# Differential attention on one core: a values product per two query blocks, head norms gathered after the loop, Fourier terms ahead of the head terms

## The chip, the cores and the metric

The kernel runs on one core of a Trainium2 chip. The metric is the device time of one execution in microseconds (us). The engines are TensorE (PE in the rows; its weight loads are PEld), VectorE (DVE), ScalarE (ACT), GpSimd (POOL) and SyncE (SP), which issues most transfers.

## The reference, cut to what matters

Two blocks run one after the other on 512 tokens of width 1024: a convolution block with an MLP, then a block of two layers. The first of these layers holds differential attention with a Fourier mixer, and only that part is touched:

```python
def diff_attend(q, k, v, lam):
    s = jnp.einsum('bqhmd,bkhmd->bhmqk', q, k).astype(jnp.float32)
    p = jax.nn.softmax(s, axis=-1)
    a = p[:, :, 0] - lam * p[:, :, 1]
    return jnp.einsum('bhqk,bkhe->bqhe', a.astype(v.dtype), v)
...
def merge_even(att, f, subln, lam_init, w_out):
    b, n = att.shape[0], att.shape[1]
    att = rmsnorm(att, subln) * (1.0 - lam_init)
    o = jnp.concatenate([att.reshape(b, n, ATTN_V_W), fourier_mix(f)], axis=-1)
    return o @ w_out
```

There are 6 heads, 512 queries, 768 keys (512 tokens and 256 of context), two score maps per head with 64 channels each, and values of 128 channels. After the heads' norm over 128 channels, 768 attention channels and 256 Fourier channels go through an output projection of 1024 x 1024. Everything is fp32. A mixture of 16 experts follows, whose weights are most of what the kernel reads.

## The kernel before

Each engine has a program of its own, written out by hand, and they meet through counting semaphores. An engine does its instructions in order, so a waiting one holds up all behind it. A plain fp32 product shows as two passes in the rows (x12 for six products), a transpose as one.

The loop over `it` = 0 to 23 takes one query block of 128 rows of one head at a time (four blocks per head). For each block:

- TensorE makes the two score maps (`scores`, L1153) into three PSUM banks, two blocks ahead; the sets of two blocks alternate in banks 0 to 5.
- DVE takes the row maxima (`softmax_max`, L1561), one block ahead.
- ACT takes the exponentials with their sums (`exps`, L772), one block ahead.
- DVE combines the two maps (`combine`, L1573 to L1583) into `attn`.
- TensorE transposes the 768 key columns in six pieces (`attn_turn`, L1167), four into bank 6 and two into the first half of bank 7.
- ACT copies them to `aT` (`turn_in`, L781 and L783).

Per head, TensorE then makes the values product of 512 queries (`values`, L1174) into bank 7, queued ahead of the transposes of the next head's first block. ACT copies it to `o_sb` and squares it (`head_out`, L790 and L791), a product with a matrix of 1/128 gives the mean over channels on all 128 partitions (`head_stat`, L1182, bank 6), ACT takes the root (`head_root`, L795, which needs another function table than the exponentials), and DVE inverts it and scales the head into `hT` (`head_norm`, L1589 and L1590). These steps of a head stand in the queues of the next head's first two blocks, as here on TensorE:

```python
                if it and it % 4 == 0:
                    values(it // 4 - 1)
                if it > 4 and it % 4 == 1:
                    head_stat(it // 4 - 1)
                attn_turn(it)
```

After the last head the output projection makes eight tiles of 8 products each (`dense`, L903), of which products 0 to 5 take the heads and 6 and 7 the Fourier channels, ready since before the loop. DVE adds each tile to `xT` (L1407), ACT squares it for the next norm, POOL sums the squares, and L933 and L936 finish that sum. SyncE loads the first expert weights into the slots of a ring (`load_experts`) after the release of all projection tiles (L408).

Of the kernel before, what the change touches and what calls it, by code (L numbers as in the profile page):

```python
# [8 lines left out]
ALU = mybir.AluOpType  # L9
# [3 lines left out]
P = 128  # L13
D = 1024
DT = D // P
# [86 lines left out]
def block_kernel(nc, A, out):  # L102
# [137 lines left out]
    with ExitStack() as ctx:  # L240
# [85 lines left out]
        o_sb = carve(arena, 7680, N)  # L326
# [24 lines left out]
        for name in (  # L351
# [7 lines left out]
            "scores", "score_half", "neg_max", "probs", "attn_ready", "attn_turned", "aT_sb", "pv_done", "o_in", "o_stat", "o_rms",  # L359
            "o_ready",  # L360
# [33 lines left out]
        def _(sp):  # L394
# [8 lines left out]
            def load_experts(layer):  # L403
# [5 lines left out]
                if layer == 0:  # L409

                    sp.wait_ge(S["pv_done"], HEADS)
# [130 lines left out]
        def _(act):  # L542
# [233 lines left out]
            def turn_in(it):  # L776
                act.wait_ge(S["attn_turned"], it + 1)
                m = it % 4
                if m == 0 and it:
                    act.wait_ge(S["pv_done"], it // 4)  # L780
                act.activation(aT[:, 0:4, m * P:(m + 1) * P], psum[:, 6, :].rearrange("p (a b) -> p a b", a=4),  # L781
                               ACT.Copy).then_inc(S["aT_sb"], 1)
                act.activation(aT[:, 4:6, m * P:(m + 1) * P], psum[:, 7, 0:256].rearrange("p (a b) -> p a b", a=2),  # L783
                               ACT.Copy).then_inc(S["aT_sb"], 1)

            def head_out(h):
                act.wait_ge(S["pv_done"], h + 1)
                if h:
                    act.wait_ge(S["o_ready"], h)
                act.activation(o_sb, psum[:, 7, :], ACT.Copy).then_inc(S["o_in"], 1)  # L790
                act.activation(sq[:, 0, :], psum[:, 7, :], ACT.Square).then_inc(S["o_in"], 1)  # L791

            def head_root(h):
                act.wait_ge(S["o_stat"], h + 1)
                act.activation(rms[:, :], psum[:, 6, :], ACT.Sqrt, bias=eps[:, 0:1]).then_inc(S["o_rms"], 1)  # L795
# [12 lines left out]

# [80 lines left out]
        def _(pe):  # L889
# [268 lines left out]
            def attn_turn(it):  # L1158
# [622 lines left out]
```

## Time and profile before

| | |
|---|---|
| Median of 3 runs | 2569.98 us (2568.38 to 2574.26) |
| The profiled execution | 2574.75 us, its span 2573.0 us |
| Granted TensorE clock, mean | 0.965 |
| Busy in the span | TensorE 92%, DVE 27%, ACT 15%, POOL 2% |
| Head loop, from the first scores to the last combination | 154.60 us |
| From there to the first pass of the projection | 16.94 us |

Busy is the time in which an engine shows an instruction. The granted clock is a share of full speed: 1.00 is 2.4 GHz and 0.50 is 1.2 GHz. A wait is put down to the event that came last before the waiting instruction began.

### The profile page before, as it was taken

How to read it: one execution, taken by the hardware profiler on the slowest of the kernel's cores; microseconds unless marked ns; L12 is line 12 of the kernel's file. 1: busy time of each engine (PE TensorE's matmuls, PEld its weight loads, DVE VectorE, ACT ScalarE, POOL GpSimd, SP SyncE). 2: the span in 40 equal slices, each digit the busy share in tenths (PEclk: the TensorE clock that was granted, in tenths of full speed). 3: DMA queues.
4: the chain of work that ended last, by engine and by line, in shares of the span. 5: the costliest groups of instructions: out<-in, count | busy, mean ns of one | idle time of the engine just before them, and what ended most of it. 6: DMA issues, size and time to landing. Idle time of an engine off the chain costs nothing.

```text
span 2573.0 us, 21612 instructions
## 1 busy us (share of the span) xinstructions
PE 2366.4 (92%) x8882; PEld 1064.3 (41%) x8882; DVE 706.7 (27%) x958; ACT 376.4 (15%) x653; POOL 61.0 (2%) x66
## 2 busy tenths in 40 slices
PE   4999899999998999776969999999899879999997
PEld 2443344444444455443434444443344344444443
DVE  2683200000004760575141111112311231111113
ACT  1314200000003211354020000000200110000000
POOL 1000100000000000000100000000000100000000
PEclk8999999999999999987989999999999989999999
DMA  8307458218600010100069999998410269999995
GB/s 291 126 34 262 147 210 302 76 65 298 225 0 0 33 66 33 66 1 0 16 256 428 417 428 428 428 429 346 152 66 0 108 255 429 428 427 428 428 428 232
DMA packets 110554, 565.58 MB, mean 220 GB/s; under 512 B 8344, under 2 KB 8734, under 8 KB 85918
## 3 DMA queue, kind: packets, MB, share of 16 engines
q1 hardware_dynamic: 105856, 563.09, 54.1%
q10 hardware_dynamic: 4638, 1.64, 0.3%
q8 instruction: 44, 0.72, 0.1%
q14 instruction: 16, 0.13, 0.0%
HBM read 562.61 MB, written 2.10 MB: 219 GB/s over the span
## 4 chain that ended last, share of the span: by engine, by line
PE 80%; DMA 9%; DVE 6%; issue 2%; ACT 2%; SPq 1%; ACTq 0%; DVEq 0%
PE psum L903 39%; PE psum L1260 18%; DMA ring<-in_moe_w_gate_dram 7%; PE psum L1319 5%; PE psum L1275 5%; PE psum L1105 2%; PE psum L947 2%; DMA ring<-in_moe_w_down_dram 1%; PE psum L991 1%; PE psum L1174 1%; PE psum L923 1%; PE psum L1153 1%; DVE rstd L1395 1%; DVE rstd L1589 1%; PE psum L1218 1%
## 5 line engine op out<-in xcount | busy, mean ns | idle before, releaser
L903 PE MATMUL psum<-hT,ring 128*128 128x512 f32 x1632 | 717.7, 600 | 23.7 <-ACT hT L610 18.4
L1260 PE MATMUL psum<-ring,arena 128*64 128x512 f32 x3072 | 671.7, 595 | 21.6 <-DMA ring<-in_moe_w_gate_dram 14.3
L903 PEld LDWEIGHTS psum<-hT,ring 128*128 128x128 f32 x1632 | 312.4, 193 | 419.5 <-issue 412.6
L1260 PEld LDWEIGHTS psum<-ring,arena 128*64 128x64 f32 x3072 | 228.5, 137 | 450.4 <-issue 448.3
L903 PE MATMUL psum<-arena,ring 128*128 128x512 f32 x640 | 275.2, 592 | 0.0
L903 PEld LDWEIGHTS psum<-arena,ring 128*128 128x128 f32 x640 | 121.6, 190 | 153.1 <-issue 153.1
L1692 DVE TENSOR_TENSOR hT<-hT,psum 128x512 f32<-128x512 f32 x128 | 88.0, 687 | 245.6 <-PE psum L1319 245.6
L1275 PE MATMUL psum<-arena 128*128 128x128 f32 x1024 | 124.4, 282 | 2.5 <-DVE arena L1699 2.5
L1275 PEld LDWEIGHTS psum<-arena 128*128 128x128 f32 x1024 | 120.3, 197 | 14.0 <-issue 14.0
L1319 PE MATMUL psum<-arena 128*128 128x512 f32 x256 | 123.2, 619 | 0.0
L1407 DVE SCALAR_TENSOR_TENSOR xT<-psum,modv,xT 128x512 f32<-128x512 f32 x32 | 24.0, 751 | 308.5 <-PE psum L903 308.5
L1673 DVE TENSOR_TENSOR arena<-psum,arena 128x512 f32<-128x512 f32 x32 | 34.1, 1064 | 215.2 <-PE psum L1260 215.2
L1500 DVE TENSOR_TENSOR arena<-arena 128x512 f32<-128x512 f32 x32 | 22.2, 692 | 244.1 <-ACT arena L705 244.1
L947 PE MATMUL psum<-ring,cpad 128*32 128x512 f32 x576 | 66.0, 611 | 16.4 <-DMA ring<-in_w_mod_dram 16.4
L1167 PE MATMUL psum<-K,arena 128*128 128x128 f32 x144 | 29.6, 354 | 48.4 <-DVE arena L1583 33.3
L1319 PEld LDWEIGHTS psum<-arena 128*128 128x128 f32 x256 | 39.4, 188 | 83.5 <-DVE hT L1692 62.9
L597 ACT ACTIVATE sq<-xT 128x512 f32<-128x512 f32 x56 | 35.2, 631 | 260.3 <-DVE xT L1407 228.8
L1474 DVE SCALAR_TENSOR_TENSOR arena<-arena,vecT 128x512 f32<-128x512 f32 x90 | 72.3, 803 | 3.2
L1687 DVE COPY arena<-psum 128x512 f32<-128x512 f32 x16 | 11.1, 692 | 214.8 <-PE psum L1260 214.8
L705 ACT ACTIVATE arena<-psum 128x512 f32<-128x512 f32 x32 | 19.1, 598 | 311.7 <-PE psum L903 311.7
L829 ACT ACTIVATE arena<-psum 128x512 f32<-128x512 f32 x16 | 9.6, 599 | 365.7 <-PE psum L1275 365.7
L1518 DVE RECIPROCAL rstd<-rms 128x512 f32<-128x512 f32 (+1 forms) x18 | 50.8, 2820 | 44.0 <-ACT rms L744 43.9
(181 smaller groups left out, 1438.3 us busy)
## 6 DMA issues: line engine op xcount, KB each, us to landing
ring<-in_moe_w_gate_dram SPq DMA_DIRECT2D x64, 2048.0 KB, 14.9
ring<-in_moe_w_up_dram SPq DMA_DIRECT2D x64, 2048.0 KB, 16.7
ring<-in_moe_w_down_dram SPq DMA_DIRECT2D x64, 2048.0 KB, 16.8
ring<-in_ada_w_dram SPq DMA_DIRECT2D x24, 2048.0 KB, 10.5
ring<-in_mlp_w_dram SPq DMA_DIRECT2D x16, 2048.0 KB, 13.0
ring<-in_w_mod_dram SPq DMA_DIRECT2D x12, 2048.0 KB, 13.2
ring<-in_conv_w_pw_dram SPq DMA_DIRECT2D x6, 2048.0 KB, 18.5
ring<-in_conv_w_in_dram SPq DMA_DIRECT2D x6, 2048.0 KB, 18.8
```

Of the source, the lines that this page charges most:

```text
L597: act.activation(sq[:, g % 2, 0:width], src[:, j, :], ACT.Square).then_inc(S["sq_ready"], 1)
L903: ins = pe.matmul(bank[:, 0:width], w[:, k, col:col + P], src(k), start=start and k == 0, stop=stop and k == kts - 1)
L947: ins = pe.matmul(psum[32 * q:32 * q + 32, MISC, :], cpad[:, k, :], ws[q][:, k, :], start=k == 0, stop=k == DT - 1, skip_group_check=True)
L1105: ins = pe.matmul(psum[:, t % 6, 0:width], src, w[:, k, 0:width], start=k == 0, stop=k == DT - 1)
L1167: ins = pe.transpose(psum[:, 6 + k // 4, (k % 4) * P:(k % 4 + 1) * P], attn[:, it % 2, k * P:(k + 1) * P], ident)
L1260: ins = pe.matmul(psum[64 * e:64 * e + 64, bank + nh, :], src[:, 4 * h + k, 64 * e:64 * e + 64], w[:, k, nh * N:(nh + 1) * N], start=h == ...
L1275: ins = pe.matmul(psum[:, 6 + half, (fj % 4) * P:(fj % 4 + 1) * P], h_tok[:, tt, fj * P:(fj + 1) * P], sel[:, tt, :, :].rearrange("p a b - ...
L1319: pe.matmul(psum[:, 6 + fj % 2, :], y_sb[:, fj * P:(fj + 1) * P], gselT, start=True, stop=True)\
L1474: ins = dve.scalar_tensor_tensor(out=acc, in0=u, scalar=w, in1=acc, op0=ALU.mult, op1=ALU.add)
L1518: link(dve.reciprocal(rstd[:, 0:w], rms[:, 0:w]))
L1673: dve.tensor_tensor(quarters(act_e[:, half, :]), psum[:, 2 + half, :].rearrange("s (p k) -> s p k", k=4), sil[:, half, :].rearrange("s (p ...
L1692: dve.tensor_tensor(hT[:, fj, :], hT[:, fj, :], psum[:, 6 + fj % 2, :], ALU.add)\
```

## The change

The head's steps are cut and spread. The values product is made for two query blocks at a time (256 columns) in the first half of bank 7, behind the first four transposes of an even block. The last two transposes of a block are a group of their own: for even blocks they go into bank 6 after ACT has copied the first four out of it, for odd blocks into the second half of bank 7. ACT writes the values straight into `hT` and squares them. The mean of squares is made by four narrow products, each for 64 queries, onto one group of 32 partitions, and ACT puts the 64 columns into `o_ms`. `o_ms` holds all heads in 768 columns; five heads' roots are taken together during block 22, the sixth's after the loop, and DVE inverts them in two instructions. `widen` spreads each head's inverse over 128 partitions and 512 queries with eight products of 64 columns, into bank 6 or 7, and `head_norm` scales `hT` in place from there. The projection (`project`) starts with the Fourier products of six tiles, placed between these steps, and then takes the head products; the two last tiles are whole. SyncE's wait for the values counts 12 instead of 6. In the diff the removed bodies of functions printed above are left out.

```diff
@@ -323,7 +323,9 @@
         prob = carve(arena, 0, 4, NK)
         attn = carve(arena, 3072, 2, NK)
         aT = carve(arena, 4608, HEADS, N)
-        o_sb = carve(arena, 7680, N)
+        o_ms = carve(arena, 8960, HEADS * P)
+        o_inv = carve(arena, 9728, HEADS * P)
+        o_parts = ((0, HEADS - 1), (HEADS - 1, HEADS))
         prob1 = carve(arena, 8192, NK)
...
@@ -773,38 +775,49 @@
                                    bias=small[:, 28 + 2 * b + m:29 + 2 * b + m],
                                    accum_out=small[:, 4 + 2 * b + m:5 + 2 * b + m]).then_inc(S["probs"], 1)
...
+            def turn_in(it, part):
+                act.wait_ge(S["attn_turned"], 2 * it + 1 + part)
+                at = (it % 4) * P
+                if part == 0:
+                    if it >= 4:
+                        act.wait_ge(S["pv_done"], it // 2 - 1)
+                    src = psum[:, 6, :].rearrange("p (a b) -> p a b", a=4)
+                    act.activation(aT[:, 0:4, at:at + P], src, ACT.Copy).then_inc(S["aT_sb"], 1)
+                else:
+                    src = (psum[:, 7, 256:512] if it % 2 else psum[:, 6, 0:256]).rearrange("p (a b) -> p a b", a=2)
+                    act.activation(aT[:, 4:6, at:at + P], src, ACT.Copy).then_inc(S["aT_sb"], 1)
+            def values_out(p):
+                h, half = divmod(p, 2)
+                act.wait_ge(S["pv_done"], p + 1)
+                act.activation(hT[:, h, 256 * half:256 * half + 256], psum[:, 7, 0:256], ACT.Copy).then_inc(S["o_in"], 1)
+                act.activation(sq[:, 0, 0:256], psum[:, 7, 0:256], ACT.Square).then_inc(S["o_in"], 1)
+            def square_mean(p):
+                act.wait_ge(S["o_stat"], p + 1)
+                act.activation(o_ms[:, 64 * p:64 * p + 64], psum[:, 7, 0:64], ACT.Copy).then_inc(S["o_ms"], 1)
+            def heads_root(part):
+                lo, hi = o_parts[part]
+                act.wait_ge(S["o_ms"], 2 * hi)
+                act.activation(o_ms[:, P * lo:P * hi], o_ms[:, P * lo:P * hi], ACT.Sqrt, bias=eps[:, 0:1])\
+                    .then_inc(S["o_rms"], 1)
             exps(0)
             for it in range(4 * HEADS):
                 if it + 1 < 4 * HEADS:
                     exps(it + 1)
-                if it and it % 4 == 0:
-                    head_out(it // 4 - 1)
-                if it > 4 and it % 4 == 1:
-                    head_root(it // 4 - 1)
-                turn_in(it)
-            head_out(HEADS - 1)
-            head_root(HEADS - 1)
+                turn_in(it, 0)
+                if it >= 2 and it % 2 == 0:
+                    values_out(it // 2 - 1)
+                turn_in(it, 1)
+                if it >= 2 and it % 2:
+                    square_mean(it // 2 - 1)
+                if it == 4 * HEADS - 2:
+                    heads_root(0)
+            values_out(2 * HEADS - 1)
+            square_mean(2 * HEADS - 1)
+            heads_root(1)
@@ -1155,56 +1168,97 @@
...
+            def attn_turn(it, part):
+                if part == 0:
+                    pe.wait_ge(S["attn_ready"], it + 1)
+                    if it:
+                        pe.wait_ge(S["aT_sb"], 2 * it - 1 + it % 2)
+                elif it % 2 == 0:
+                    pe.wait_ge(S["aT_sb"], 2 * it + 1)
+                elif it > 1:
+                    pe.wait_ge(S["o_in"], it - 1)
+                for k in ((0, 1, 2, 3), (4, 5))[part]:
+                    at = (k % 4) * P + (256 if part and it % 2 else 0)
+                    ins = pe.transpose(psum[:, 7 if part and it % 2 else 6, at:at + P],
                                        attn[:, it % 2, k * P:(k + 1) * P], ident)
                 ins.then_inc(S["attn_turned"], 1)
...
+            def values(p):
+                h, half = divmod(p, 2)
+                pe.wait_ge(S["aT_sb"], 4 * p + 4)
+                if p:
+                    pe.wait_ge(S["o_ms"], p)
                 for k in range(6):
+                    ins = pe.matmul(psum[:, 7, 0:256], vtok[:, k, h * P:(h + 1) * P],
+                                    aT[:, k, 256 * half:256 * half + 256], start=k == 0, stop=k == 5,
+                                    skip_group_check=True)
                 ins.then_inc(S["pv_done"], 1)
...
+            def values_stat(p):
+                pe.wait_ge(S["o_in"], 2 * p + 2)
+                for q in range(4):
+                    ins = pe.matmul(psum[32 * q:32 * q + 32, 7, 0:64], const("ones_v")[:, 0:32],
+                                    sq[:, 0, 64 * q:64 * q + 64], start=True, stop=True, skip_group_check=True)
+                ins.then_inc(S["o_stat"], 1)
+            def widen(h):
+                pe.wait_ge(S["o_inv"], 1 if h < o_parts[0][1] else 2)
+                if h < 2:
+                    pe.wait_ge(S["aT_sb"], 8 * HEADS)
+                    pe.wait_ge(S["o_ms"], 2 * HEADS)
+                else:
+                    pe.wait_ge(S["o_ready"], h - 1)
+                for half in range(2):
+                    for q in range(4):
+                        at = P * h + 64 * half
+                        ins = pe.matmul(psum[:, 6 + h % 2, 256 * half + 64 * q:256 * half + 64 * q + 64],
+                                        ident[:, 32 * q:32 * q + 1].to_broadcast([P, P]), o_inv[:, at:at + 64],
+                                        start=True, stop=True, skip_group_check=True)
+                ins.then_inc(S["o_wide"], 1)
+            def project(j, ks):
+                t = T_WO + j
+                w = arrived(pe, B_WO[j // 4])
+                for k in ks:
+                    if j == 0 and k < HEADS:
+                        pe.wait_ge(S["o_ready"], k + 1)
+                    ins = pe.matmul(psum[:, t % 6, :], w[:, k, (j % 4) * P:(j % 4 + 1) * P], hT[:, k, :],
+                                    start=k == HEADS, stop=k == HEADS - 1, skip_group_check=True)
+                if ks[-1] == HEADS - 1:
+                    ins.then_inc(S["tile_done"], 1)
             scores(0)
             scores(1)
             for it in range(4 * HEADS):
                 if it + 2 < 4 * HEADS:
                     scores(it + 2)
-                if it and it % 4 == 0:
-                    values(it // 4 - 1)
-                if it > 4 and it % 4 == 1:
-                    head_stat(it // 4 - 1)
-                attn_turn(it)
-            values(HEADS - 1)
-            head_stat(HEADS - 1)
+                attn_turn(it, 0)
+                if it >= 2:
+                    if it % 2 == 0:
+                        values(it // 2 - 1)
+                    else:
+                        values_stat(it // 2 - 1)
+                attn_turn(it, 1)
+            values(2 * HEADS - 1)
+            pe.wait_ge(S["probs"], 8 * HEADS)
+            project(0, (6, 7))
+            values_stat(2 * HEADS - 1)
+            project(1, (6, 7))
+            widen(0)
+            widen(1)
+            for j in range(2, 6):
+                project(j, (6, 7))
+                widen(j)
             for j in range(DT):
-                t = T_WO + j
-                if j == 0:
-                    pe.wait_ge(S["aT_sb"], 8 * HEADS)
-                    pe.wait_ge(S["o_rms"], HEADS)
-                    pe.wait_ge(S["o_ready"], HEADS)
+                if j >= 6:
+                    begin(T_WO + j)
+                    project(j, (6, 7, 0, 1, 2, 3, 4, 5))
                 else:
-                    begin(t)
-                w = arrived(pe, B_WO[j // 4])
-                dense(t, w, (j % 4) * P, lambda k: hT[:, k, :], DT).then_inc(S["tile_done"], 1)
+                    project(j, (0, 1, 2, 3, 4, 5))
             for part in range(2):
                 summed_stat(FFN0, part)
@@ -1579,26 +1633,30 @@
                 dve.tensor_scalar(prob1[:, N:NK], prob[:, 2 * b + 1, 0:NC], w, None, ALU.mult)
                 link(dve.tensor_scalar(prob1[:, 0:N], prob[:, 2 * b + 1, NC:NK], w, None, ALU.mult))
                 if it >= 2:
-                    dve.wait_ge(S["attn_turned"], it - 1)
+                    dve.wait_ge(S["attn_turned"], 2 * it - 2)
                 dve.scalar_tensor_tensor(out=attn[:, b, :], in0=prob[:, 2 * b, :], scalar=small[:, 8 + 4 * b:9 + 4 * b],
                                          in1=prob1, op0=ALU.mult, op1=ALU.add)\
                     .then_inc(S["attn_ready"], 1)
+            def invert_roots(part):
+                lo, hi = o_parts[part]
+                dve.wait_ge(S["o_rms"], part + 1)
+                dve.reciprocal(o_inv[:, P * lo:P * hi], o_ms[:, P * lo:P * hi]).then_inc(S["o_inv"], 1)
             def head_norm(h):
-                dve.wait_ge(S["o_rms"], h + 1)
-                link(dve.reciprocal(rstd[:, :], rms[:, :]))
-                dve.scalar_tensor_tensor(out=hT[:, h, :], in0=o_sb, scalar=gqk[:, 2:3], in1=rstd[:, :], op0=ALU.mult,
-                                         op1=ALU.mult).then_inc(S["o_ready"], 1)
-                dve.wait_ge(S["o_ready"], h + 1)
+                dve.wait_ge(S["o_wide"], h + 1)
+                dve.scalar_tensor_tensor(out=hT[:, h, :], in0=hT[:, h, :], scalar=gqk[:, 2:3], in1=psum[:, 6 + h % 2, :],
+                                         op0=ALU.mult, op1=ALU.mult).then_inc(S["o_ready"], 1)
             softmax_max(0)
             for it in range(4 * HEADS):
                 if it + 1 < 4 * HEADS:
                     softmax_max(it + 1)
                 combine(it)
-                if it > 4 and it % 4 == 1:
-                    head_norm(it // 4 - 1)
-            head_norm(HEADS - 1)
+            invert_roots(0)
+            invert_roots(1)
+            for h in range(HEADS):
+                head_norm(h)
             for j in range(DT):
                 add_to_x(T_WO + j, modv[:, 1, 16:24], j)
             scale(FFN0, xT, hT, gain[:, 4, :])
```

## Rows read from the trace of the kernel before

**Rows 1.** The page, chain of work that ended last, by line.

```profile
PE psum L903 39%; PE psum L1260 18%; DMA ring<-in_moe_w_gate_dram 7%; PE psum L1319 5%; PE psum L1275 5%; PE psum L1105 2%; PE psum L947 2%; DMA ring<-in_moe_w_down_dram 1%; PE psum L991 1%; PE psum L1174 1%; PE psum L923 1%; PE psum L1153 1%; DVE rstd L1395 1%; DVE rstd L1589 1%; PE psum L1218 1%
```

**Rows 2.** Windows, loop and projection: start:end, length, busy per engine, clock, DMA, GB/s.

```profile
1052.04:1206.64 154.60, 103.59 (x400) 62.98 (x400) 117.23 (x178) 85.57 (x167) 0.00 (x0) 0.83 0.04 14
...
1223.58:1281.36 57.78, 57.78 (x129) 25.49 (x130) 5.26 (x7) 4.42 (x7) 7.58 (x6) 0.95 0.00 0
```

**Rows 3.** Timeline of DVE in the loop: start us, duration us, what.

```profile
1072.71 1.75 DVE L1561 TENSOR_REDUCE small<-psum 128x2 f32<-128x1536 f32 x1
...
1076.87 1.75 DVE L1561 TENSOR_REDUCE small<-psum 128x2 f32<-128x1536 f32 x1
...
1080.09 1.02 DVE L1583 SCALAR_TENSOR_TENSOR arena<-arena,small 128x768 f32<-128x768 f32 x1
1086.88 3.35 DVE L1589 RECIPROCAL rstd<-rms 128x512 f32<-128x512 f32 x1 [5.77 <-ACT rms L795]
...
1194.96 3.35 DVE L1589 RECIPROCAL rstd<-rms 128x512 f32<-128x512 f32 x1 [5.88 <-ACT rms L795]
...
1202.37 1.02 DVE L1583 SCALAR_TENSOR_TENSOR arena<-arena,small 128x768 f32<-128x768 f32 x1
```

**Rows 4.** Timeline of TensorE in the loop, at the full clock.

```profile
1072.85 0.88 PE L1167 MATMUL psum<-K,arena 128*128 128x128 f32 x6 [1.79 <-DVE arena L1583]
1073.66 1.56 PE L1153 MATMUL psum<-ring 64*128 64x256 f32 x8
1075.15 5.42 PE L1174 MATMUL psum<-arena,ring 128*128 128x512 f32 x12
```

**Rows 5.** Timeline of ACT at a head's end.

```profile
1082.97 0.91 ACT L772 ACTIVATE arena<-psum,small 128x768 f32<-128x768 f32 x1
...
1084.87 1.28 ACT L795 ACT_TABLE_LOAD   x1
...
1087.88 0.60 ACT L781 ACTIVATE arena<-psum 128x512 f32<-128x512 f32 x1 [1.03 <-PE psum L1167]
1088.38 0.38 ACT L783 ACTIVATE arena<-psum 128x256 f32<-128x256 f32 x1
```

**Rows 6.** Windows inside the loop (clock before the DMA share).

```profile
1060.00:1064.00 4.00, 4.00 (x14) 2.79 (x14) 3.83 (x7) 2.48 (x6) 0.00 (x0) 0.50 0.00 0
1068.20:1072.40 4.20, 2.37 (x14) 1.68 (x14) 4.03 (x8) 2.79 (x8) 0.00 (x0) 1.00 0.00 0
...
1087.00:1095.00 8.00, 2.34 (x14) 1.65 (x14) 7.76 (x9) 2.76 (x4) 0.00 (x0) 0.85 0.01 2
...
1203.00:1209.00 6.00, 3.08 (x12) 2.28 (x12) 2.54 (x6) 2.95 (x8) 0.00 (x0) 0.50 0.00 0
```

**Rows 7.** Waits of SyncE, 1000 to 1345: total us, times, longest.

```profile
SPq L408 <- PE psum L903: 229.9, 2, 202.5
```

**Rows 8.** Timeline of TensorE elsewhere: 256, 512, 16 and 128 columns.

```profile
1011.00 7.07 PE L1105 MATMUL psum<-ring 128*128 128x256 f32 x32
...
1017.90 13.90 PE L903 MATMUL psum<-hT,ring 128*128 128x512 f32 x32
...
1299.79 0.42 PE L1227 MATMUL psum<-K,arena 16*128 16x16 f32 x4 [0.18 <-DVE arena L1613]
...
1363.12 3.74 PE L1275 MATMUL psum<-arena 128*128 128x128 f32 x32
```

**Rows 9.** Timeline of the loop's start, TensorE, then DVE.

```profile
1061.41 2.93 PE L1153 MATMUL psum<-ring 64*128 64x256 f32 x8
...
1067.62 1.02 DVE L1583 SCALAR_TENSOR_TENSOR arena<-arena,small 128x768 f32<-128x768 f32 x1
```

**Rows 10.** Groups by line and shape: count, busy us, mean ns.

```profile
L744 ACT ACTIVATE rms<-psum,eps 128x512 f32<-128x512 f32 x12 | 8.3, 691 | 0.4 <-PE psum L1072 0.4
...
L1518 DVE RECIPROCAL rstd<-rms 128x512 f32<-128x512 f32 x12 | 40.2, 3353 | 30.5 <-ACT rms L744 30.4
...
L1518 DVE RECIPROCAL rstd<-rms 128x256 f32<-128x256 f32 x6 | 10.5, 1753 | 13.6 <-ACT rms L744 13.5
```

More of the change, by code:

```diff
@@ L358, in block_kernel @@
             "qk_stat", "qk_rms", "qk_normed", "qk_rot", "qk_done",
[L359 to L360 removed]
+            "scores", "score_half", "neg_max", "probs", "attn_ready", "attn_turned", "aT_sb", "pv_done", "o_in", "o_stat", "o_ms",
+            "o_rms", "o_inv", "o_wide", "o_ready",
             "soft_exp", "aff_ready", "pos_ready", "acc_zero",
@@ L774, in exps @@
                                    accum_out=small[:, 4 + 2 * b + m:5 + 2 * b + m]).then_inc(S["probs"], 1)
[L776 to L784, printed above, removed]
@@ L1156, in scores @@
                         ins.then_inc(S["scores" if at else "score_half"], 1)
-            def attn_turn(it):
-                pe.wait_ge(S["attn_ready"], it + 1)
-                if it:
-                    pe.wait_ge(S["aT_sb"], 2 * it)
-                if it > 4 and it % 4 == 1:
-                    pe.wait_ge(S["o_rms"], it // 4)
-                for k in range(6):
-                    if k == 4 and it and it % 4 == 0:
-                        pe.wait_ge(S["o_in"], 2 * (it // 4))
-                    ins = pe.transpose(psum[:, 6 + k // 4, (k % 4) * P:(k % 4 + 1) * P],
+            def attn_turn(it, part):
[10 more added lines that the diff above has]
+                    ins = pe.transpose(psum[:, 7 if part and it % 2 else 6, at:at + P],
@@ L1168, in attn_turn @@
                                        attn[:, it % 2, k * P:(k + 1) * P], ident)
                 ins.then_inc(S["attn_turned"], 1)
-            def values(h):
-                pe.wait_ge(S["aT_sb"], 8 * h + 8)
+            def values(p):
[3 more added lines that the diff above has]
+                    pe.wait_ge(S["o_ms"], p)
                 for k in range(6):
-                    ins = pe.matmul(psum[:, 7, :], vtok[:, k, h * P:(h + 1) * P], aT[:, k, :], start=k == 0,
-                                    stop=k == 5)
+                    ins = pe.matmul(psum[:, 7, 0:256], vtok[:, k, h * P:(h + 1) * P],
+                                    aT[:, k, 256 * half:256 * half + 256], start=k == 0, stop=k == 5,
+                                    skip_group_check=True)
@@ L1176, in values @@
                 ins.then_inc(S["pv_done"], 1)
-            def head_stat(h):
-                pe.wait_ge(S["o_in"], 2 * h + 2)
-                pe.wait_ge(S["aT_sb"], min(2 * (4 * h + 5), 8 * HEADS))
-                pe.matmul(psum[:, 6, :], const("ones_v"), sq[:, 0, :], start=True, stop=True)\
-                    .then_inc(S["o_stat"], 1)
+            def values_stat(p):
[4 more added lines that the diff above has]
+                ins.then_inc(S["o_stat"], 1)
```

12 lines of the change are left out of this document (1 added, 11 removed).

## The prediction

> **What bounds the kernel now.** I read the chain that ended last first: TensorE's dense products and expert products hold most of it, and the attention lines L1153, L1167, L1174 and the DVE reciprocal L1589 are small entries in it [rows 1]. The change touches only attention and the start of the output projection, so I then cut the span into stretches [rows 2]. The head loop takes 154.60 us (1052.04 to 1206.64), and in it TensorE works 103.59, DVE 117.23 and ACT 85.57: no engine fills it, so something makes them wait in turn. A tail of 16.94 follows to 1223.58, and then 57.78 of solid projection.
>
> The timeline of DVE shows what [rows 3]. Inside a head one query block costs one DVE period: one row maximum starts at 1072.71 and the next at 1076.87, so 4.16 us with no gap. At each head's end DVE stops: the combination that starts at 1080.09 ends at 1081.11, and its next instruction, the reciprocal of the head norm, starts at 1086.88, 5.77 later. From that reciprocal to the one four heads on (1194.96) is 108.08, so 27.02 a head, where four blocks at 4.16 would be 16.64. The other 10.4 us are the values product of 512 columns [rows 4], two evacuations and a table load with a square root on ACT [rows 5], the DVE reciprocal of 3.35, and TensorE restarting at the half clock after it idled (granted 1.00 inside a head, 0.85 in 1087 to 1095, 0.50 at 1203) [rows 6]. All of it lies between two instructions of one queue.
>
> Where a saving here would go: SyncE's loads of the expert weights wait for the projection's products (L408 behind L903) [rows 7]. Everything after the projection therefore moves with its end, and I count a microsecond saved before it as one saved.
>
> **The new loop.** DVE's part of a block is unchanged, 4.16, and the norm leaves it. I call C the end of an even block's combination and follow what is released, with starts from [rows 4]. TensorE starts 0.05 after a combination. Six transposes take 0.81 to the next start (1072.85 to 1073.66), 0.135 each: the first four 0.54. Now the values product comes behind them: 12 passes of 256 columns at 7.07 / 32 = 0.22 (I use 0.215, half of the 0.429 of a 512-column pass: 13.90 for 32, less the last one's 0.59, over 31) [rows 8]: 2.58. Two transposes: 0.27. Then the scores of the block three ahead: 1.56 to their end, and 0.05 to DVE. Sum 5.05 after C.
>
> DVE meanwhile does one block and wants these scores at C + 4.08. They are 0.97 late. From them to the end of the combination is 4.24 (1076.87 to 1081.11) [rows 3]. So two blocks take 5.05 + 4.24 = 9.29, against 8.32 by DVE alone. Behind the waiting transposes on TensorE's queue stand exactly these scores; that is the new wait's price.
>
> Does ACT hold it up? After C it copies four transposes (0.60), waits for the values (C + 3.34), takes two 256-column copies (0.38 each) and the two last transposes, to C + 4.3, then the exponentials of the next block (2 x 0.91, 0.2 for the read-out) to C + 6.2 [rows 5]. DVE wants these at C + 7.04: 0.8 spare. The mean over squares (8 narrow passes) is not in the trace; I take 0.5, bounds 0 and 8 x 0.112 = 0.9, and it lies where TensorE has 1.2 us to spare: free. TensorE's sum per pair is 2 x 1.49 + 2 x 0.81 + 2.58 + 0.5 = 7.7 of 9.29.
>
> **Start and end of the loop.** At block 0 the last two transposes must wait for ACT's copy, as they reuse its bank. The scores of block 3 slip by about 0.7 (a copy 0.60 and a release), at the half clock as now [rows 6, 9]. Block 2's combination ends now at 1068.64 [rows 9]; new 1069.35. Ten pairs to block 22: 1069.35 + 92.9 = 1162.25. It now ends at 1203.39 [rows 3]. Gain there 41.1.
>
> **The tail, counted from block 22's end.** Now the projection's last pass is at 1281.36 [rows 2], 77.97 later. New, in order: ACT turns the block in by 4.3 and at once loads the root's table and takes the root of 640 columns, 1.28 + 0.80 (0.69 at 512 [rows 10], and 0.86 ns for each column more, as 0.60 and 0.38 of the copies give it [rows 5]): 6.35. Block 23's copies stand behind that in ACT's queue, end at 7.2, and the mean of the pair before at 7.45. The last values product runs 7.45 to 10.03; the Fourier terms of tile 0, 4 passes, 1.72, to 11.75; squares mean 0.5; tile 1's terms to 13.97. Beside this DVE inverts 640 columns from 6.35 (6.25 ns a column and 0.15 by its 512 and 256 forms [rows 10]: 4.15) and the last 128 (0.95) by 14.0. That is hidden; without the products before it, it would cost about 3.
>
> Widening is new work for TensorE: per head 8 products of 64 columns, 16 passes with 128-column weights. No row has that shape. Upper neighbour: passes of 128 columns at (3.74 - 0.27) / 31 = 0.112; lower: 16-column passes at (0.42 - 0.21) / 3 = 0.07 [rows 8]. I take 0.112, because both load weights of 128 columns for a plain product: 1.79 a head, 10.7 for six; with 0.07, 6.7. A bound above: if weights and columns went one after the other, 0.112 + 0.056 = 0.17, 16.1.
>
> Beside this stands the Trainium skill, page "TensorE: Matmul & The Clock Gate", part 3, "The mechanism": it lets a weight load overlap a running product only when the row groups differ, which here they do not. By that rule the six heads would cost about 5 us more than I take. The trace disagrees: the 32 passes of L1275 share all rows, each with its own load, and still come every 0.112.
>
> Go on: widen 0 and 1 to 17.6; four times 1.72 + 1.79, to 31.6; the six head terms of six tiles, 6 x 12 x 0.429 = 30.9, to 62.5; two whole tiles, 13.7: 76.2. DVE's six normalisations from PSUM (0.75 each) fit between two widenings. The projection's own passes are the same 128 as now, only reordered. Now they lose 2.8 to the half clock at their start (57.78 against 128 x 0.429 = 54.9) [rows 2]; the new tail has no idle above 1.8 us. The tail thus gives 77.97 - 76.2 = 1.8: the Fourier terms hide the norm chain, but the widening eats nearly all they hide.
>
> **Sum.** 41.1 + 1.8 = 42.9. The profiled execution took 2574.75; 2574.75 - 42.9 = 2531.8. The median shown is 2569.98, 4.8 below that execution, so I forecast 2527.
>
> **The rivals.**
> Forecast, pairs at 9.3 and full clock: chance 0.70; 2527, own range 2519 to 2534 (widening 4 less to 5 more, runs 3 either way).
> DVE alone sets the loop, 8.32 a pair: ten times 0.97 more, 2517. For it: DVE is the only engine that is full in a head. Against: the queue order puts the scores behind the values. Chance 0.07.
> The clock drops in part of the loop or the tail. A pair at the half clock is bound by TensorE, about 2 x 7.5 = 15 (a score set took 2.93 there against 1.56 [rows 9, 4]), so 5.5 more each; after a short one the engine is full and recovers, as in 1060 to 1064, where 4.00 of 4.00 preceded the rise [rows 6]. Two or three pairs: 2540. Chance 0.13.
> Other side: the half clock in the whole loop. Ten pairs at 15 instead of 9.29 add 57, and the time is 2584, slower by 14. It decides from 13.6 a pair on, where the 42.9 are gone. Against: at 2.37 of 4.20 busy the clock stayed 1.00 [rows 6], and the new loop is busier. Chance 0.04.
> The Trainium skill's same page, "A second HAM failure mode: psum-queue depth-cycling", describes this oscillation for groups of products with short idles between banks; the trace so far shows idles of 1.8 us per block without it.
> No difference: the gain is absorbed behind the projection. The weights' loads wait for the projection [rows 7], so I see nothing to absorb it. Chance 0.03, 2570. The 0.03 left over is for a wait I have not seen, a gain of 15 to 30.
>
> The range 2515 to 2543 takes in the first three. A measurement of this kernel tells about 0.2%, 5 us, from no change: faster 0.93, same 0.03, slower 0.04.
>
> **What would show it.** DVE's row maxima alternate 4.16 and about 5.1 apart, the longer one released by TensorE's L1153 form; no reciprocal of 512 columns in the loop; no table load between the first exponential and block 22; clock 1.00 from about 1065 on; block 23's combination ends near 1164; six groups of 16 short passes of 1.8; the last projection pass near 1238. I am wrong if a pair takes over 10 us, if the clock falls in the loop, or if the widening passes come slower than 0.17.

## The result, and the profile after

| | before | after |
|---|---|---|
| Median | 2572.11 us (4 runs, 2568.38 to 2574.26) | 2529.88 us (4 runs, 2529.26 to 2530.17) |
| Profiled execution, its span | 2574.75, 2573.0 us | 2530.17, 2528.4 us |
| First scores to the last combination | 154.60 us | 112.86 us |
| First scores to the first pass after the projection | 229.32 us | 188.59 us |
| Granted TensorE clock, mean | 0.965 | 0.977 |
| The same, in the stretch of the fourth row | 0.85 | 0.97 |

The ratio after to before is 0.9837, with a 95% interval of 0.982 to 0.9854. The kernel became 42 us faster; 2527 was forecast, inside a range of 2515 to 2543.

The fourth row is the measure used from here on, since all that the change touches lies in it: from the first pass of `scores` to the first pass of the product that finishes the next norm, which stands behind the last projection pass. Before it ran from 1052.04 to 1281.36 [rows 2].

**The loop.** This is TensorE's timeline after; the lines have moved, so that L1166 is `scores`, L1183 the transposes, L1193 the values product and L1202 the mean over squares. It answers to [rows 4].

```profile
1079.40 0.66 PE L1183 MATMUL psum<-K,arena 128*128 128x128 f32 x4 [1.66 <-DVE arena L1637]
1079.89 2.75 PE L1193 MATMUL psum<-arena,ring 128*128 128x256 f32 x12
1082.48 0.38 PE L1183 MATMUL psum<-K,arena 128*128 128x128 f32 x2
1082.80 1.56 PE L1166 MATMUL psum<-ring 64*128 64x256 f32 x8
1084.29 0.66 PE L1183 MATMUL psum<-K,arena 128*128 128x128 f32 x4
1084.87 0.32 PE L1202 MATMUL psum<-sq,K 128*32 128x64 f32 x8
```

The first four transposes begin when a combination ends, 12 passes of 256 columns take 2.59 to the next start, and the scores stand behind them, to 1084.36. DVE's timeline (after, answering to [rows 3]) shows who waits for that:

```profile
1075.10 1.76 DVE L1615 TENSOR_REDUCE small<-psum 128x2 f32<-128x1536 f32 x1 [0.90 <-PE psum L1166]
...
1079.26 1.75 DVE L1615 TENSOR_REDUCE small<-psum 128x2 f32<-128x1536 f32 x1
...
1084.40 1.76 DVE L1615 TENSOR_REDUCE small<-psum 128x2 f32<-128x1536 f32 x1 [0.91 <-PE psum L1166]
```

The row maxima come 4.16 and 5.14 apart, and the later one of a pair was released by the scores after 0.91 of idle. Nothing else stops DVE from 1066 to block 22. The norm's reciprocal of 3.35 and the stop of 5.77 at each head's end [rows 3] are gone.

**The tail.** DVE ends block 22 at 1163.19 (1162.17 and 1.02). TensorE's timeline from there to the end of the projection; L1229 is `project` and L1217 `widen`:

```profile
1163.24 0.66 PE L1183 MATMUL psum<-K,arena 128*128 128x128 f32 x4 [3.15 <-DVE arena L1637]
...
1167.61 0.63 PE L1183 MATMUL psum<-K,arena 128*128 128x128 f32 x4 [0.90 <-ACT arena L788]
...
1170.62 4.51 PE L1193 MATMUL psum<-arena,ring 128*128 128x256 f32 x12 [1.77 <-ACT arena L798]
1174.94 1.92 PE L1229 MATMUL psum<-hT,ring 128*128 128x512 f32 x4
...
1177.03 1.98 PE L1229 MATMUL psum<-hT,ring 128*128 128x512 f32 x4
1178.86 3.68 PE L1217 MATMUL psum<-arena,K 128*128 128x64 f32 x32
1182.37 1.94 PE L1229 MATMUL psum<-hT,ring 128*128 128x512 f32 x4
...
1196.39 44.85 PE L1229 MATMUL psum<-hT,ring 128*128 128x512 f32 x104
1241.08 1.02 PE L946 MATMUL psum<-rms,K 128*128 128x512 f32 x2
```

TensorE has no gap from 1170.62 on. But the same 12 passes that took 2.75 in the loop take 4.51 here. The windows of after (TensorE, weight loads, DVE, ACT, POOL, then the granted clock) say why:

```profile
1065.00:1160.00 95.00, 78.01 (x489) 58.04 (x487) 81.65 (x141) 60.60 (x151) 0.00 (x0) 1.00 0.00 1
...
1166.00:1170.60 4.60, 1.96 (x19) 1.15 (x18) 0.96 (x1) 3.92 (x8) 0.00 (x0) 1.00 0.00 0
1170.60:1175.00 4.40, 4.38 (x13) 3.55 (x14) 3.19 (x1) 0.00 (x0) 0.00 (x0) 0.61 0.00 0
1171.60:1175.00 3.40, 3.40 (x10) 2.65 (x9) 2.19 (x1) 0.00 (x0) 0.00 (x0) 0.50 0.00 0
...
1196.40:1241.00 44.60, 44.60 (x106) 19.80 (x106) 6.00 (x8) 4.41 (x7) 7.60 (x6) 1.00 0.00 0
```

From 1065 to 1160 the clock is full, where [rows 6] has 0.85 and 0.50 at a head's end; only in the loop's first blocks, from 1059.0 to 1065.8, is it at the half level, as it was before. Behind block 22 it falls once, from 1171.6 to 1175.0, which is most of the last values product, behind a stretch in which TensorE was busy 1.96 of 4.60. The projection then runs at 1.00, against 0.95 in [rows 2].

### The profile page after: what moved, and what is told of

Read it like the earlier page. It is cut to its first block, busy times and chain, and to the rows that moved or that the text cites. A ratio compares the mean times of both kernels' runs of the same rounds, so it can differ in the third digit from the quotient of the medians.

```text
span 2528.4 us, 22132 instructions
## 1 busy us (share of the span) xinstructions
PE 2354.4 (93%) x9134; PEld 1077.1 (43%) x9134; DVE 691.6 (27%) x954; ACT 362.1 (14%) x663; POOL 61.0 (2%) x66
## 4 chain that ended last, share of the span: by engine, by line
PE 81%; DMA 9%; DVE 5%; issue 2%; ACT 1%; SPq 1%; ACTq 0%; DVEq 0%
PE psum L916 37%; PE psum L1314 18%; DMA ring<-in_moe_w_gate_dram 8%; PE psum L1373 5%; PE psum L1329 5%; PE psum L1118 2%; PE psum L960 2%; PE psum L1229 2%; PE psum L1004 1%; DMA ring<-in_moe_w_down_dram 1%; PE psum L1193 1%; PE psum L936 1%; DVE small L1615 1%; DVE rstd L1449 1%; PE psum L1166 1%
## 5 line engine op out<-in xcount | busy, mean ns | idle before, releaser
L916 PEld LDWEIGHTS psum<-hT,ring 128*128 128x128 f32 x1504 | 287.1, 192 | 381.5 <-issue 374.7
L1745 DVE COPY arena<-psum 128x512 f32<-128x512 f32 x16 | 11.1, 692 | 214.2 <-PE psum L1314 214.2
L1229 PE MATMUL psum<-hT,ring 128*128 128x512 f32 x128 | 56.5, 595 | 0.0
```

Source lines behind the costliest of these rows:

```text
L916: ins = pe.matmul(bank[:, 0:width], w[:, k, col:col + P], src(k), start=start and k == 0, stop=stop and k == kts - 1)
L1229: ins = pe.matmul(psum[:, t % 6, :], w[:, k, (j % 4) * P:(j % 4 + 1) * P], hT[:, k, :], start=k == HEADS, stop=k == HEADS - 1, skip_group_ ...
```

## The experiments

Seven variants of the kernel after were run, and that kernel once more beside them. Diffs are against it. "Stretch" is the measure named above, from each kernel's own trace. The first four shared one chip (before had a median of 2572.44 there), the last four another (2571.33).

| | median us (lowest to highest) | ratio to before, 95% | stretch us |
|---|---|---|---|
| after, again | 2530.33 (2529.9 to 2531.7) | 0.984 (0.9824 to 0.9857) | 188.58 |
| scores ahead of the values product | 2519.68 (2514.62 to 2520.3) | 0.9792 (0.9775 to 0.9808) | 177.63 |
| Fourier terms after the widening | 2540.28 (2539.22 to 2544.26) | 0.9883 (0.9867 to 0.99) | 199.77 |
| one values product per head | 2536.99 (2535.21 to 2540.25) | 0.9863 (0.9846 to 0.9879) | 195.44 |
| two Fourier tiles before block 22's transposes | 2525.48 (2523.79 to 2527.77) | 0.9825 (0.9811 to 0.9838) | 185.33 |
| the widening in one run | 2530.62 (2530.11 to 2531.11) | 0.9843 (0.9827 to 0.9858) | 191.52 |
| scores first and Fourier in the gap | 2516.64 (2512.1 to 2516.83) | 0.9785 (0.9771 to 0.9798) | 173.32 |
| scores first in TensorE's queue alone | 2540.19 (2539.66 to 2541.85) | 0.9883 (0.9867 to 0.9898) | 199.67 |

**The kernel after, again.** No edit. It gives the measure's own spread: 188.58 against 188.59.

> The changed kernel once more, as the measure for the other runs beside it. Theory: 2529.9 within 1 us; a pair of blocks 9.31 us, the last combination about 112 us after the first scores.

The stretch repeats to 0.01 here. But in one later kernel block 22's values product, with the same code and the same idle ahead of it, fell to the half clock and took 1.7 longer. So a difference of 2 in one trace is not yet one of the edit.

**Scores ahead of the values product.** The forecast says that a pair costs 9.29 and not 8.32 because the scores stand behind the values product. So they are put ahead of it:

```diff
-            scores(0)
-            scores(1)
+            for it in range(3):
+                scores(it)
             for it in range(4 * HEADS):
-                if it + 2 < 4 * HEADS:
-                    scores(it + 2)
                 attn_turn(it, 0)
-                if it >= 2:
-                    if it % 2 == 0:
-                        values(it // 2 - 1)
-                    else:
-                        values_stat(it // 2 - 1)
+                if it % 2 == 0:
+                    if it + 3 < 4 * HEADS:
+                        scores(it + 3)
+                elif it >= 2:
+                    values_stat(it // 2 - 1)
                 attn_turn(it, 1)
+                if it % 2 and it + 3 < 4 * HEADS:
+                    scores(it + 3)
+                if it >= 2 and it % 2 == 0:
+                    values(it // 2 - 1)
```

On ACT `values_out` moves with it, to the odd block ahead of its `turn_in`.

> The changed kernel with one order altered: on TensorE the scores of the block three ahead stand before the values product of an even block instead of behind it, and ACT takes the values out one block later. Theory (the wait of DVE for those scores, 0.9 us a pair, is the whole price of the values product in the loop): pairs fall from 9.31 to DVE's own 8.32, ten pairs, so 9.9 us less, about 2520. Rival (ACT or the release of bank 7 is next in line at once, so that DVE waits for exponentials instead): pairs stay above 9, less than 4 us gained, 2526 to 2530.

DVE's timeline of this kernel:

```profile
1103.03 1.75 DVE L1617 TENSOR_REDUCE small<-psum 128x2 f32<-128x1536 f32 x1
...
1107.19 1.75 DVE L1617 TENSOR_REDUCE small<-psum 128x2 f32<-128x1536 f32 x1
...
1111.35 1.75 DVE L1617 TENSOR_REDUCE small<-psum 128x2 f32<-128x1536 f32 x1
```

Every 4.16, with no wait at all. The stretch is 10.96 shorter. Of that 10.0 lie in the loop, where ten pairs at 0.97 would be 9.7: block 22's transposes begin 100.7 after the first scores instead of 110.7. The rest lies behind them. So the 0.97 late in each pair was this place in the queue, and not the length of TensorE's work.

**The same order in TensorE's queue alone.** Same diff without ACT's part.

> The scores ahead of the values product on TensorE, but ACT's order left as in the changed kernel: it takes the values out before it copies the last two transposes and before the next exponentials. Theory (ACT then waits for the later values product and hands DVE the exponentials late): exponentials done 7.9 us after the even block's combination where DVE wants them at 6.1, so a pair takes 10.1, ten times 0.8 above the changed kernel: 2538. Rival (ACT's place in the loop has slack enough): as with both orders altered, 2520.

DVE's timeline:

```profile
1093.74 1.75 DVE L1617 TENSOR_REDUCE small<-psum 128x2 f32<-128x1536 f32 x1
...
1097.67 0.17 DVE L1629 RECIPROCAL small<-small 128x2 f32<-128x2 f32 x1 [1.97 <-ACT arena L774]
...
1103.99 1.75 DVE L1617 TENSOR_REDUCE small<-psum 128x2 f32<-128x1536 f32 x1
```

A pair takes 10.25. ACT's timeline of the same kernel shows what DVE waits for:

```profile
1094.87 0.38 ACT L793 ACTIVATE hT<-psum 128x256 f32<-128x256 f32 x1 [3.85 <-PE psum L1193]
...
1095.41 0.39 ACT L788 ACTIVATE arena<-psum 128x256 f32<-128x256 f32 x1
1095.68 0.92 ACT L774 ACTIVATE arena<-psum,small 128x768 f32<-128x768 f32 x1
```

ACT stood at the values product, which is now made later, and the next block's exponentials are queued behind its copies. The stretch is 11.1 longer than in the kernel after and 22.0 longer than with both orders moved. On TensorE the edit is a gain only when ACT's queue moves too; ACT's part alone was not run.

**One values product per head.** This takes back one part of the change, the product for two blocks, and keeps the gathered norms. Queue order is the one of before: the values product ahead of the next head's first transposes.

```diff
-            def values(p):
-                h, half = divmod(p, 2)
-                pe.wait_ge(S["aT_sb"], 4 * p + 4)
+            def values(h):
+                pe.wait_ge(S["aT_sb"], 8 * h + 8)
...
-                    ins = pe.matmul(psum[:, 7, 0:256], vtok[:, k, h * P:(h + 1) * P],
-                                    aT[:, k, 256 * half:256 * half + 256], start=k == 0, stop=k == 5,
-                                    skip_group_check=True)
+                    ins = pe.matmul(psum[:, 7, :], vtok[:, k, h * P:(h + 1) * P], aT[:, k, :], start=k == 0,
+                                    stop=k == 5, skip_group_check=True)
```

> The changed kernel with the values product of a whole head again (512 columns, once in four blocks, ahead of the transposes as before the change), the norms still gathered after the loop. It tells the worth of gathering the norms from that of halving the product. Theory (gathering removes the chain of root and reciprocal from the queues and is nearly all of the gain): four blocks take 16.64 + about 2.5 against 18.62, so 2 to 6 us more than the changed kernel, 2532 to 2536. Rival (the halved product is what keeps TensorE's queue short): four blocks above 22 us, over 15 us more, above 2545.

DVE's timeline, the first row maxima of two heads:

```profile
1104.61 1.76 DVE L1613 TENSOR_REDUCE small<-psum 128x2 f32<-128x1536 f32 x1 [2.55 <-PE psum L1165]
...
1123.89 1.76 DVE L1613 TENSOR_REDUCE small<-psum 128x2 f32<-128x1536 f32 x1 [2.55 <-PE psum L1165]
```

A head takes 19.28, against 27.02 before [rows 3] and 2 x 9.30 = 18.6 after. Gathering the norms, with the new tail that it needs, is worth most of the change: 229.32 - 195.44 = 33.9 of the 40.7. Halving the product, with its new place in the queue, gives the other 6.9, of which 0.7 x 5 = 3.4 lie in the loop and most of the rest at its end: here the last values product has 512 columns and takes 7.31, with the clock at 0.50 until 1177.9, against 4.51. The shares hold in this order; the halved product without the gathered norms was not run. Nor does a run part the 33.9 into the waits themselves and the clock that they let fall: the mean in the stretch was 0.85 before and 0.93 here.

**Fourier terms after the widening.** All 96 widening passes come first, and each tile of the projection is made whole.

```diff
-            project(0, (6, 7))
             values_stat(2 * HEADS - 1)
-            project(1, (6, 7))
-            widen(0)
-            widen(1)
-            for j in range(2, 6):
-                project(j, (6, 7))
+            for j in range(6):
                 widen(j)
...
```

> The changed kernel with the Fourier products back inside their tiles: the twelve products no longer stand between the steps of the norm chain. Theory (they only cover the chain from the last values product to the first widening and the last normalisation): the values' copies, mean and copy are exposed, 1.5 us, and the last head's normalisation, 0.8, so 2 to 3 us more, about 2532.5. Rival (the cover also keeps the clock up, or the chain is longer than I worked out): 5 us more or over, with the six widenings at the half clock, 2535 to 2540.

TensorE's timeline, then three windows of this kernel:

```profile
1169.39 4.51 PE L1193 MATMUL psum<-arena,ring 128*128 128x256 f32 x12 [1.76 <-ACT arena L798]
1174.74 0.32 PE L1202 MATMUL psum<-sq,K 128*32 128x64 f32 x8 [0.84 <-ACT sq L794]
1175.49 19.21 PE L1217 MATMUL psum<-arena,K 128*128 128x64 f32 x96 [0.42 <-ACT arena L798]
1194.49 12.08 PE L1229 MATMUL psum<-hT,ring 128*128 128x512 f32 x24
```

```profile
1173.73:1177.14 3.41, 2.15 (x24) 1.87 (x24) 0.95 (x1) 1.28 (x4) 0.00 (x0) 1.00 0.02 5
1177.14:1194.49 17.35, 17.35 (x84) 17.35 (x83) 3.74 (x5) 0.00 (x0) 0.00 (x0) 0.50 0.00 0
...
1194.50:1200.00 5.50, 5.50 (x11) 2.43 (x12) 0.75 (x1) 0.00 (x0) 0.00 (x0) 0.72 0.00 0
```

The idle that the Fourier products had filled is only 0.84 and 0.42 here. Yet the stretch is 11.2 longer. 19.00 to the next start for 96 passes is 0.198 each in the mean instead of 0.110. The clock was full when the row of narrow passes began (1175.49), behind 3.41 of which TensorE was busy 2.15. It fell 1.65 later, stood at 0.50 for the other 17.35, with TensorE shown busy all the time, and came back at 1197.6, among the 512-column products. At the low level a pass took about 0.21, by an estimate: some 15 passes fit into the 1.65 at 0.11 each, which leaves 81 for 17.35.

**The widening in one run, behind the Fourier products.** This parts two readings of that run: that a row of narrow passes brings the clock down whatever stands before it, or that it fell because of the idles just ahead.

```diff
-            project(1, (6, 7))
-            widen(0)
-            widen(1)
-            for j in range(2, 6):
+            for j in range(1, 6):
                 project(j, (6, 7))
+            for j in range(6):
                 widen(j)
```

> The changed kernel with the Fourier products of all six tiles ahead of the first widening, so that all six widenings (96 passes of 64 columns) run in a row and start at the full clock. The same products in the same number. Theory (the half clock in the kernel with the Fourier terms last came from the idle before the widenings, and narrow products keep a clock that is high): 10.5 us at clock 1.00, no difference from 2530.3 beyond 1 us. Rival (narrow products in a row do not hold the clock, whatever came before; the wide products between them do): the clock falls to 0.50 within the row, up to 8 us more, 2534 to 2538.

TensorE's timeline, then two windows:

```profile
1161.28 4.44 PE L1193 MATMUL psum<-arena,ring 128*128 128x256 f32 x12
...
1169.85 5.46 PE L1193 MATMUL psum<-arena,ring 128*128 128x256 f32 x12 [1.77 <-ACT arena L798]
1175.11 2.25 PE L1229 MATMUL psum<-hT,ring 128*128 128x512 f32 x4
...
1177.54 8.85 PE L1229 MATMUL psum<-hT,ring 128*128 128x512 f32 x20
1186.22 10.83 PE L1217 MATMUL psum<-arena,K 128*128 128x64 f32 x96
```

```profile
1162.20:1165.60 3.40, 3.40 (x10) 2.58 (x9) 0.70 (x1) 0.00 (x0) 0.00 (x0) 0.50 0.00 0
...
1187.00:1192.00 5.00, 5.00 (x47) 5.00 (x46) 1.76 (x3) 0.00 (x0) 0.00 (x0) 1.00 0.00 0
```

The same 96 passes take 10.67 to the next start, 0.111 each, at 1.00. Both rows began at the full clock. With 8.85 of wide products right ahead it held; behind idles of 0.84 and 0.42 it fell inside the row. So the row by itself does not bring it down. That the idles do is what the two traces suggest, one of each. The median is that of after. The stretch is 2.9 longer. 1.7 of it are block 22's values product (1161.28), which ran at the half clock here and took 2.76 in after, though neither the code up to there nor the idle ahead of it (3.15) differs. The other 1.3 lie in the last values product and the Fourier products behind it, which stayed at the low clock for longer.

**Two Fourier tiles before block 22's transposes.** The tail begins with 3.15 of idle before 1163.24, then 0.90 and 1.77. The products of two tiles, ready since before the loop, are put into the first of these.

```diff
                     scores(it + 2)
+                elif it == 4 * HEADS - 2:
+                    pe.wait_ge(S["probs"], 2 * it + 2)
...
+                    project(0, (6, 7))
+                    project(1, (6, 7))
                 attn_turn(it, 0)
...
```

Further down the products of tiles 2 and 3 take the places of those of 0 and 1, and those of 4 and 5 theirs.

> The changed kernel with the Fourier products of tiles 0 and 1 moved ahead of block 22's transposes, where TensorE stood idle for 3.15 us. Theory (that idle and the next two let the clock fall, so that the last values product took 4.3 us instead of 2.6; and the two products, 3.4 us, are taken off the tail): 3.4 + 1.7 less, minus 0.3 by which the transposes are late, about 2525.5. Rival (the clock falls all the same, because of the later idles of 0.9 and 1.8): 3 us less, 2527.

TensorE's timeline:

```profile
1158.60 3.70 PE L1229 MATMUL psum<-hT,ring 128*128 128x512 f32 x8
...
1166.45 0.63 PE L1183 MATMUL psum<-K,arena 128*128 128x128 f32 x4 [0.90 <-ACT arena L788]
...
1169.46 4.51 PE L1193 MATMUL psum<-arena,ring 128*128 128x256 f32 x12 [1.76 <-ACT arena L798]
```

The stretch is 3.3 shorter: the 3.70 of products moved into the idle, and that is all. The last values product still took 4.51, so the 3.15 of idle was not needed for the fall. The median's gain of 4.4 can't be told from 3.3 by its spread.

Nor do the 0.90 and 1.77 settle it. In the kernel with the order changed in TensorE's queue alone, the same work stood between much the same idles (the window from 1178.00 to 1182.90):

```profile
1179.93 0.63 PE L1183 MATMUL psum<-K,arena 128*128 128x128 f32 x4 [1.12 <-ACT arena L788]
...
1182.94 2.83 PE L1193 MATMUL psum<-arena,ring 128*128 128x256 f32 x12 [1.76 <-ACT arena L798]
```

```profile
1178.00:1182.90 4.90, 2.06 (x18) 1.16 (x16) 0.94 (x1) 3.92 (x8) 0.00 (x0) 1.00 0.00 0
```

TensorE was busy for no greater share there than in the 4.60 of after, and the last values product ran at the full clock. In that trace the clock had fallen earlier, in an idle of 2.78 that ended at 1171.91, and was back at 1178.0. So like idles were followed by either level.

**Both together.** Scores first in both queues, and a Fourier tile on either side of block 22's first transposes. In the kernel with scores first alone, TensorE's timeline had this there:

```profile
1153.14 0.66 PE L1183 MATMUL psum<-K,arena 128*128 128x128 f32 x4 [1.77 <-DVE arena L1639]
1154.48 0.69 PE L1183 MATMUL psum<-K,arena 128*128 128x128 f32 x2 [0.69 <-ACT arena L785]
1154.96 4.22 PE L1193 MATMUL psum<-arena,ring 128*128 128x256 f32 x12
```

Two idles and then a values product at the half clock, as in the tail of after. The edit, beside the one above:

```diff
+                if it == 4 * HEADS - 2:
+                    pe.wait_ge(S["probs"], 2 * it + 2)
...
+                    project(0, (6, 7))
                 attn_turn(it, 0)
+                if it == 4 * HEADS - 2:
+                    project(1, (6, 7))
...
```

> The scores ahead of the values product, as before, and in block 22 the Fourier products of tile 0 ahead of the transposes and of tile 1 between their two groups. Theory: the two effects add: 2519.7, minus 3.4 for the products, minus 1.6 for the values product of the half clock, plus 1.0 by which the second group of transposes is late, 2515.7. Rival (what is taken off the tail is given back in ACT's or DVE's chain of roots and inverses, which then sets the start of the widenings): 2518 to 2520.

TensorE's timeline of the kernel with both:

```profile
1154.18 1.88 PE L1229 MATMUL psum<-hT,ring 128*128 128x512 f32 x4
...
1156.12 2.76 PE L1193 MATMUL psum<-arena,ring 128*128 128x256 f32 x12
...
1160.99 2.83 PE L1193 MATMUL psum<-arena,ring 128*128 128x256 f32 x12 [0.68 <-ACT arena L798]
```

With the idles filled the same product takes 2.76; the clock is full from 1070 to the end of the projection. That fits the view that the fall needs such idles, but it is one trace of each, and block 22's product took 2.76 in after and 4.44 in the kernel with the widening in one run, behind the same idle. The last values product, behind 0.68, takes 2.83 in both. The stretch is 173.32, 15.3 below after and 4.3 below scores first alone: 3.4 are the two tiles taken off the tail. 2516.64 is the lowest median of all, but its interval overlaps that of scores first alone.

## Why the prediction was right

**The loop pair, right.** Forecast 5.05 + 4.24 = 9.29, measured 9.30 (1075.10 to 1084.40). The longer interval was released by the scores, as named. Its terms: 12 passes of 256 columns 2.59 for 2.58, the scores 0.91 late for 0.97. The mean over squares took 0.25 to the next start (1084.87 to 1085.12) where I took 0.5; it was covered either way. ACT did not hold DVE up. Moving the scores ahead brought the pair to the 8.32 of the rival "DVE alone", which had the right price and the wrong queue order.

**Start and end of the loop, right.** Block 22 ends at 1163.19, 110.70 after the first scores at 1052.49. Before it was 151.35 (1203.39 less 1052.04). The gain is 40.65; forecast 41.1.

**The tail, mis-sized.** The step "the tail thus gives 1.8" failed. From block 22's end to the end of the projection it takes 77.89 (1163.19 to 1241.08), against 77.97 before: 0.1. Part by part:

| from block 22's end | forecast | measured |
|---|---|---|
| last values product begins | 7.45 | 7.43 |
| it ends | 10.03 | 11.75 |
| Fourier terms, mean and widening end | 31.6 | 33.20 |
| projection ends | 76.2 | 77.89 |

The 1.7 is the last values product, 4.32 to the next start instead of 2.58; what the other parts miss cancels. Idle times were as forecast, 1.77 the longest behind block 22's transposes; what failed is the step from "no idle above 1.8 us" to no half clock. I took it from the loop, where one such idle comes per block or pair and the clock holds. Here 0.90 and 1.77 fell into one stretch of 4.60 with 1.96 of work. What exactly brings the clock down stays open. Filling the 3.15 of idle ahead of both changed nothing (4.51 again). Filling 1.77 and 0.69 with wide products went with a values product of 2.76 instead of 4.22. But idles of 1.12 and 1.76 were followed by a product at the full clock (2.83), and one and the same product behind 3.15 of idle took 2.76 in one kernel and 4.44 in another. So such idles let the clock fall in some traces and not in others, and the term should have been a range: from nothing to 2.7 for a values product that meets the low level (5.26 to the next start in the kernel with the widening in one run, 1169.85 to 1175.11).

**The widening, right.** 32 passes from 1178.86 to 1182.37 are 3.51, so 1.755 a head for 1.79, and 0.110 a pass. The Trainium skill, page "TensorE: Matmul & The Clock Gate", part 3, "The mechanism", lets a weight load overlap a running product where the row groups do not conflict, and I had set that against the rows. The trace disagrees with it as a limit: each pass uses all 128 rows and has its own 128-column load, and one by one they would have given 0.17, the bound above. The same sentence of the page also allows the overlap by way of the background weight buffer, which I had left out; with that the trace agrees.

**Fourier first, right for too small a reason.** I said that it hides the norm chain, "about 3". The run without it lost 11.2. The idle it left open was 1.3; the rest is the clock, which fell 1.65 into the widening and stayed low: 96 x (0.198 - 0.110) = 8.4 over the row, and about 1.6 in the first projection passes, at the half level for 3.13 more (1194.49 to 1197.62). In the changed kernel the Fourier products fill these idles. They do not bring the clock back: it rose at 1175.0, when the first of them had just begun (1174.94), and in the run without them at 1173.7.

**The clock in the loop, right.** 1.00 from 1065 to 1160 with TensorE busy 78.01 of 95.00. The same page's section "A second HAM failure mode: psum-queue depth-cycling" describes an oscillation for groups of products with short idles; the loop has an idle of 1.66 in each pair and does not show it. The rival with half the clock in all pairs, the one on the other side, is out.

**The sum.** Forecast 42.9. The stretch gave 40.7 (40.65 and 0.08). The two profiled executions differ by 44.58, so 3.9 more lie outside it, where the code is the same. From 2574.75 I came to 2531.8, and the profiled execution of after took 2530.17: 2.2 more for tail and loop, 3.9 less from outside. Then I took off 4.8 more, since the median of before was that much under its profiled execution; for the kernel after the median is only 0.3 under its own. That is how 2527 stands 2.9 below 2529.88: 2.2 and 4.5 on one side, 3.9 on the other. That it came so near is in part luck; the loop's 40.65 for 41.1 is not.

## What to carry to other kernels

When a chain of several engines sits once per head in queues that otherwise run in step, take it out of the loop and do it once for all heads: 34 of the 41 us came from that, with ready products laid over the chain. Then look at which instruction the full engine waits for and what stands ahead of it in its queue; moving it one place was worth 11 us more, but only with the partner engine's order changed as well (it lost 11 us without). And fill the short idles ahead of a long row of narrow passes: behind wide products the row took 10.7 us, behind idles of 0.84 and 0.42 it took 19.0, since the clock fell inside it and did not come back before the row's end. This last rests on one trace of each.

## What the runs showed that was not expected

A row of narrow passes that TensorE is shown busy with throughout can run at either clock. Both rows of 96 passes of 64 columns with 128-column weights began at 1.00. One held it for its 10.7 us; in the other it fell to 0.50 after 1.65 us and stayed there for 17.35 us of unbroken work. The busy share in the profile therefore does not tell the clock. It rose 3.1 us into the products of 512 columns behind that row. Elsewhere it rose without any: in the kernel with two Fourier tiles ahead of block 22's transposes it was back at 1173.6, still in the values product of 256 columns.

The expert layers, whose code is the same in all these kernels, differ between traces. From the first pass after the projection to the last pass of the same product one layer on it is 759.0 in before (1281.4 to 2040.4), 755.6 in after (1241.1 to 1996.7), and 758.8 in the kernel with one values product per head (1247.4 to 2006.2). In the other seven traces it lies between 754 and 757. The profiled execution of before, on which my sum stands, has the long form, and this is nearly all of the 3.9 above. What makes it was not tried and stays open.
